# Linear attention's small products in the banks of scores and transposes, weights' splits in another order, head norms by logarithm and exponential

## The chip, the cores and the metric

One core of one Trainium2 chip. The metric is the device time of one execution in microseconds (us), the median of 3 runs; less is better.

## The reference, cut to what matters

Two transformer blocks in fp32 on 512 positions of width 1024. The first has forgetting attention and differential attention. The output of the latter is normed for each head, `y * rsqrt(mean(y*y) + eps) * gain`, and gated. The second block has block attention with relative positions (`moba_attention`) and gated linear attention side by side, then a cross attention to 256 memory rows and a 4096-wide MLP. The part that the change is about:

```python
def body(S, inp):                     # gated linear attention, one chunk
    qi, ki, vi, gi = inp
    b = jnp.cumsum(gi.astype(jnp.float32), axis=2)
    o_inter = jnp.einsum('bhcd,bhde->bhce', qf * jnp.exp(b), S)
    ...
    A = jnp.einsum('bhid,bhjd,bhijd->bhij', qf, kf, decay)
    o_intra = jnp.einsum('bhij,bhje->bhie', A, vf)
    ...
o_g = rms_norm_2(o_g, g_norm[l]).reshape(B, T, G_WIDTH) * jax.nn.silu(rg)
```

There are 4 heads with keys of 64 and values of 128.

## The kernel before

Five engines run their own instruction lists, written out by hand and tied by semaphores; `Plan` only counts groups and steps, so that each engine knows which value of a semaphore to wait for. There is no scheduler: an engine does its list in order, and whatever stands behind a waiting instruction waits too.

**Large products.** fp32 products are made of three float32r matmuls (`three`, lines 748 to 750): high by high, low by high, high by low. Weights come in halves of 512 KB through two raw buffers (`w_raw`, issued by SP's queue, line 561). ScalarE writes each half's high part (`split_hi`, line 1243), VectorE its low part (`split_lo`, by `lo_part`, line 1855) into four slots. A raw buffer is loaded again when VectorE has made the low part of the half before the last; a slot is free when the product that used it is done. `next_hi(name, n)` and `next_lo(name, n)` split the half four places behind half n of `name`. A product is either `t_product` (one half, one bank, 24 matmuls of 512 columns) or `m_quarters` (four halves, four banks, 24 matmuls for each quarter; `behind(q)` issues other work after quarter q). All of them write the four PSUM banks `lin` in turn: `claim(g)` makes TensorE wait until the group four before it has been read.

**Scores, transposes, head sums.** Four other banks, `sc` and `tr` with two each, hold attention scores and transposed probabilities; `sum_bank(h)` names them as four. They are used by the attentions, by the transposes of a norm's output and by the head sums (`head_sum`, line 797), and not by linear attention's products.

**Linear attention.** The four tiles of 128 positions are handled at once. `cross` (line 1085) computes the score blocks between different tiles, 6 for each head, in two groups for each head. Inside a tile a block is found on seven levels, `LEVELS = [64, 32, 16, 8, 4, 2, 1]`, and an eighth for the diagonal: at each level VectorE makes the distances to the middle of each block (`level_distance`, lines 2206 and 2207), ScalarE their exponential (`level_exp`, line 1607), VectorE the operands (`level_operands`, lines 2217 and 2218), TensorE 16 products of 128 by 128 with 64 rows (line 1105), and VectorE copies each head's entries under the level's mask into `g_a` (`level_scores`, line 2226). Ahead of all this stands the decay's logarithm: ScalarE takes an exponential on line 1326 and a logarithm on line 1327, and the first exponential after it on line 1611. Both `cross` and `levels` are groups of `lin`. Between levels stand large products, `rg` after each odd level and `ka2` after levels 2 and 4. The two `qa2` products stand ahead of `cross`. After the levels come `gla_pv` (line 1118, scores times values), and then `va2`, with two head sums behind each of its quarters 0 and 1.

**The order of splits around it.** VectorE makes the distances of levels 0 to 3 and the operands of levels 0 and 1 first, and then the four low parts due during `vg`. ScalarE has its high parts behind the exponentials, too, and the copies of `vg` to `g_v` behind the third one.

**Head norms.** For each of the two (in the first block for `y_1` of differential attention, in the second for linear attention) ScalarE squares the heads (line 1335), TensorE sums over partitions by a product with ones, ScalarE takes the square root (`head_roots`, line 1343), VectorE inverts it (line 1943) and multiplies (line 1944). There are two buffers for roots, so ScalarE's third and fourth root wait for the first two products of VectorE. In the second block ScalarE then waits for all four (`y_norm` 8), and only then come the splits and value tiles of `va2` (`v_heads`, lines 1353 and 1936), on both engines, ahead of the block attention's loop. In that loop each step has a score, an exponential, transposes of an earlier step, and a part of a large product as filling.

## Time and profile before

| | |
|---|---|
| Median of 3 runs | 1315.74 us (1313.95 to 1317.02) |
| The profiled execution's own time | 1315.0 us |
| Its span | 1313.2 us, mean granted clock 0.981 |
| TensorE busy (matmuls) | 1237.2 us, 94% |
| VectorE busy | 696.9 us, 53% |
| ScalarE busy | 549.6 us, 42% |
| Largest named wait of VectorE | 237.6 us before `w_lo`, for ScalarE's `w_hi` |

The profile names PE for TensorE's matmuls, PEld for its weight loads, DVE for VectorE, ACT for ScalarE, POOL for GpSimd. Times run from the span's start. An idle time is put down to the instruction that came last before it ended. Idle time on an engine that is not the bottleneck costs nothing.

### The profile page before, as it was taken

The numbers are of one execution on the slowest core, as the hardware profiler recorded it, in microseconds if no ns is written. First come the engines' busy times: TensorE is split into PE (matmuls) and PEld (weight loads), VectorE is DVE, ScalarE is ACT, GpSimd is POOL, SyncE is SP. The second block draws the span as 40 slices with busy tenths as digits, with TensorE's granted clock in tenths as the row PEclk, the third lists the DMA queues.
The fourth block names the chain that finished last, engine by engine and source line by source line (L and its number), as shares of the span: only waits on it lengthen the run. The fifth ranks groups of instructions, "written<-read, shape, count | busy, mean of one in ns | idle before, by whom it ended". The sixth has DMA issues, their size and how long they took to land.

```text
span 1313.2 us, 16539 instructions
## 1 busy us (share of the span) xinstructions
PE 1237.2 (94%) x6162; PEld 1026.9 (78%) x6162; DVE 696.9 (53%) x1047; ACT 549.6 (42%) x943; POOL 119.0 (9%) x193
## 2 busy tenths in 40 slices
PE   7999999999999989788888999999999999999996
PEld 5877887777888787666677789887798888888885
DVE  5556566865333557463657657444654343443433
ACT  5456685654332434422266545342343232231321
POOL 2023122200000010000014110010000000000000
PEclk9999999999999999899989999999999999999999
DMA  5312233113334342331023145510323332323321
GB/s 175 102 49 59 71 97 96 32 34 96 97 97 158 113 162 54 92 113 48 17 64 113 65 144 163 160 62 16 97 85 108 97 96 96 96 97 96 95 96 64
DMA packets 148227, 120.64 MB, mean 92 GB/s; under 512 B 4866, under 2 KB 123714, under 8 KB 148163
## 3 DMA queue, kind: packets, MB, share of 16 engines
q1 hardware_dynamic: 142672, 106.05, 27.1%
q10 hardware_dynamic: 5490, 13.73, 3.0%
q8 instruction: 41, 0.67, 0.2%
q14 instruction: 24, 0.19, 0.0%
HBM read 115.55 MB, written 4.22 MB: 91 GB/s over the span
## 4 chain that ended last, share of the span: by engine, by line
PE 80%; DVE 11%; ACT 4%; DMA 2%; issue 2%; POOL 0%; ACTq 0%; DVEq 0%; SPq 0%
PE lin L748 24%; PE lin L750 23%; PE lin L749 23%; DVE w_lo L1855 2%; PE tr L904 2%; DMA x_m<-in_x 1%; ACT w_hi L1243 1%; PE sc L914 1%; DVE g_z L1943 1%; DVE t_r L1943 1%; PE sc L916 1%; PE tr L897 1%; DMA w_raw<-in_w_in 1%; PE lin L940 1%; DVE neg_max L1880 1%
## 5 line engine op out<-in xcount | busy, mean ns | idle before, releaser
L1855 DVE TENSOR_TENSOR w_lo<-w_raw,w_hi 128x1024 fp32r<-128x1024 f32 x194 | 237.4, 1229 | 248.4 <-ACT w_hi L1243 237.6
L748 PE MATMUL lin<-h_hi,w_hi 128*128 128x512 f32 (+1 forms) x848 | 328.8, 388 | 23.5 <-DVE v_hl L1936 8.2
L750 PE MATMUL lin<-h_hi,w_lo 128*128 128x512 f32 (+1 forms) x848 | 320.4, 378 | 0.0
L749 PE MATMUL lin<-h_lo,w_hi 128*128 128x512 f32 (+1 forms) x848 | 320.4, 378 | 0.0
L1243 ACT ACTIVATE w_hi<-w_raw 128x1024 fp32r<-128x1024 f32 x194 | 203.8, 1054 | 244.3 <-PE lin L750 145.9
L748 PEld LDWEIGHTS lin<-h_hi,w_hi 128*128 128x128 f32 x848 | 162.4, 191 | 53.5 <-DVE v_hl L1936 8.4
L750 PEld LDWEIGHTS lin<-h_hi,w_lo 128*128 128x128 f32 x848 | 162.2, 191 | 29.6
L749 PEld LDWEIGHTS lin<-h_lo,w_hi 128*128 128x128 f32 x848 | 162.7, 192 | 25.5 <-issue 0.2
L748 PE MATMUL lin<-w_hi,u_hi 128*128 128x512 f32 x256 | 99.6, 389 | 0.0
L749 PE MATMUL lin<-w_lo,u_hi 128*128 128x512 f32 x256 | 99.6, 389 | 0.0
L750 PE MATMUL lin<-w_hi,u_lo 128*128 128x512 f32 x256 | 99.6, 389 | 0.0
L1880 DVE TENSOR_REDUCE neg_max<-sc 128x1 f32<-128x128 f32 (+3 forms) x112 | 52.3, 478 | 76.7 <-PE sc L916 57.0
L748 PE MATMUL lin<-w_hi,h_hi 128*128 128x512 f32 x192 | 77.8, 405 | 4.4 <-DVE h_lo L1855 4.2
L750 PE MATMUL lin<-w_hi,h_lo 128*128 128x512 f32 x192 | 75.7, 394 | 0.0
L749 PE MATMUL lin<-w_lo,h_hi 128*128 128x512 f32 x192 | 75.7, 394 | 0.0
L1285 ACT ACTIVATE p<-sc,neg_max 128x128 f32<-128x128 f32 (+1 forms) x80 | 42.2, 527 | 76.9 <-DVE neg_max L1880 75.1
L623 POOL TENSOR_SCALAR p<-p,rden 128x128 f32<-128x128 f32 (+1 forms) x80 | 53.8, 673 | 163.4 <-DVE rden L1884 115.2
L750 PEld LDWEIGHTS lin<-w_hi,u_lo 128*128 128x128 f32 x256 | 48.1, 188 | 10.0
L748 PEld LDWEIGHTS lin<-w_hi,u_hi 128*128 128x128 f32 x256 | 48.1, 188 | 9.9
L749 PEld LDWEIGHTS lin<-w_lo,u_hi 128*128 128x128 f32 x256 | 48.1, 188 | 9.9
L2449 DVE SCALAR_TENSOR_TENSOR u_f<-lin,relu 128x512 f32<-128x512 f32 x32 | 22.1, 691 | 61.3 <-ACT relu L1789 61.3
L617 POOL TENSOR_TENSOR rstd<-var,minus_half 128x1 f32<-128x1 f32 x22 | 13.0, 593 | 446.2 <-DVE var L1835 446.2
(300 smaller groups left out, 1943.8 us busy)
## 6 DMA issues: line engine op xcount, KB each, us to landing
w_raw<-in_w_in SPq DMA_DIRECT2D x74, 512.0 KB, 3.9
w_raw<-in_w_up SPq DMA_DIRECT2D x32, 512.0 KB, 4.0
w_raw<-in_w_down SPq DMA_DIRECT2D x32, 512.0 KB, 3.6
w_raw<-in_w_out SPq DMA_DIRECT2D x16, 512.0 KB, 3.6
w_raw<-in_w_xkv SPq DMA_DIRECT2D x16, 512.0 KB, 4.0
w_raw<-in_w_branch SPq DMA_DIRECT2D x8, 512.0 KB, 3.7
w_raw<-in_w_xq SPq DMA_DIRECT2D x8, 512.0 KB, 4.2
w_raw<-in_w_xo SPq DMA_DIRECT2D x8, 512.0 KB, 3.6
```

The lines of the kernel that those rows point to most:

```text
L623: pool.tensor_scalar(p, p, rden[:, s:s + 1], 1.0, ALU.mult, ALU.mult).then_inc(s_norm, 1)
L748: pe.matmul(o, lh, rh, start=start, stop=False)
L749: pe.matmul(o, lh, rl, start=False, stop=False)
L750: return pe.matmul(o, ll, rh, start=False, stop=stop)
L897: mm = pe.transpose(tr[:, r % 2, P * b:P * b + P], src[:, c:c + P], ident[:, :])
L904: mm = pe.transpose(tr[:, r % 2, P * j:P * j + P], src(j), ident[:, :])
L1243: act.activation(w_hi[u % SLOTS][:, :], w_raw[u % 2][:, :], ACT.Copy).then_inc(w_hi_s, 1)
L1285: act.activation(p, sc[:, s % 2, 0:n], ACT.Exp, bias=neg_max[:, s:s + 1], accum_out=denom[:, s:s + 1]).then_inc(s_exp, 1)
L1855: return dve.tensor_tensor(out, x, as_f32(hi), ALU.subtract)
L1880: dve.reduce_max(neg_max[:, s:s + 1], sc[:, s % 2, 0:n], AX, negate=True).then_inc(s_max, 1)
L1943: link(dve.reciprocal(root[:, h % 2, :], root[:, h % 2, :]))
L2449: dve.scalar_tensor_tensor(u, bank(g), 0.0, r, ALU.max, ALU.mult).then_inc(dve_evac, 1)
```

## The change

- `cross`, `levels` and `gla_pv` leave the groups of `lin`. They write `sum_bank(0)` to `sum_bank(3)`, and have semaphores of their own (`cross_done`, `cross_read`, `level_done`, `level_read`, `pv_done`, `pv_read`).
- TensorE's order: `cross` of two heads ahead of each `qa2` product, a large product behind each of levels 0 to 5 (`ka2`, `rg`, `ka2`, `rg`, `rg`, `rg`), level 6 ahead of `va2`, the diagonal level behind `va2`'s quarter 0, `gla_pv` behind quarter 1, all four head sums behind quarter 2.
- VectorE makes the low parts due during `vg` between the distances and operands; in the levels the masked copies come first, then the split and the rest of `ka2` or `qa2`, then operands and distances. ScalarE has two high parts ahead of the first exponentials.
- Head norms: `exp(-0.5 * ln(mean + eps))` on ScalarE, for four heads each function in turn, written over the squares. VectorE only multiplies. In the second block the square is read from PSUM, the gating with `g_gain` moves into steps 2 to 5 of the block attention's loop, and two of VectorE's norms stand behind its value tiles.

```diff
@@
     return fill, head


-KEYS_IN_LEVEL = {2: 0, 4: 1}
+BEHIND_LEVEL = [("ka2", 0), ("rg", 0), ("ka2", 1), ("rg", 1), ("rg", 2), ("rg", 3)]
 BY_TILES = [(0, 0), (0, 1), (1, 0), (1, 1), (0, 2), (0, 3), (1, 2), (1, 3)]

@@
-    p.group("cross", "A", 8)
-    for lev in range(len(LEVELS) + 1):
-p.group("levels", "D", 4)
-if lev % 2 == 1:
-    p.t_halves("rg", "A")
-elif lev in KEYS_IN_LEVEL:
-    p.t_halves("ka2", "AD")
-    p.group("gla_pv", "A", 4)
+    for name, _ in BEHIND_LEVEL:
+p.t_halves(name, "A" if name == "rg" else "AD")
     p.m_quarters("va2", "AD")
     p.attention("moba_pv", "AD", 32, 1, "moba")
@@
     def head_sum(h, squares, n):

         pe.wait_ge(sq_t, 4 * n + h + 1)
+        if n == 1:
+            pe.wait_ge(pv_read, h + 1)
         pe.matmul(sum_bank(h), ones[:, :], squares, start=True, stop=True).then_inc(sum_t, 1)

@@ TensorE @@
-    t_groups("qa2", 0, 2, hh, hl)
-    pe.wait_ge(gz_done, 1)
-    for h in range(4):
+    def cross_scores(h):
+
         rows = slice(HD * (h % 2), HD * (h % 2) + HD)
         kd, kx, qe = B["g_kd"][rows, h // 2, :], B["g_kx"][rows, h // 2], B["g_qe"][rows, h // 2, :]
...
-            g = G["cross"][2 * h + part]
-            claim(g)
-            for n, (key, i) in enumerate(pairs):
-                mm = pe.matmul(lin[:, g % 4, P * n:P * n + P], key, qe[:, P * i:P * i + P],
+            n = 2 * h + part
+            if n >= 4:
+                pe.wait_ge(cross_read, n - 3)
+            for c, (key, i) in enumerate(pairs):
+                mm = pe.matmul(sum_bank(n % 4)[:, P * c:P * c + P], key, qe[:, P * i:P * i + P],
                                start=True, stop=True)
-            mm.then_inc(lin_step, 1)
-    for lev in range(len(LEVELS) + 1):
+            mm.then_inc(cross_done, 1)
+    def level_products(lev):
+
+        if lev < len(LEVELS):
+            pe.wait_ge(gz_done, lev + 2)
...
+            heads = (2 * pair, 2 * pair + 1)
+            for h in heads:
+                if lev == 0:
+                    pe.wait_ge(cross_read, 5 + h)
                 else:
-                    keys_l.append(B["g_k"][rows, h // 2, :])
-                    queries_l.append(B["g_q"][rows, h // 2, :])
+                    pe.wait_ge(level_read, 4 * (lev - 1) + h + 1)
...
+                    mm = pe.matmul(sum_bank(h)[:, c], k[:, c], q[:, c], start=True, stop=True)
...
-                        mm.then_inc(lin_step, 1)
-        if lev % 2 == 1:
-            t_product("rg", lev // 2, 0, KT, hh, hl)
-        elif lev in KEYS_IN_LEVEL:
-            t_product("ka2", KEYS_IN_LEVEL[lev], 0, KT, hh, hl)
...
+                        mm.then_inc(level_done, 1)
+
+    def gla_values():
+        for h in range(4):
+            pe.wait_ge(cross_read, 8)
+            pe.wait_ge(level_read, 4 * len(LEVELS) + h + 1)
+            for j in range(NT):
+                mm = pe.matmul(sum_bank(h)[:, P * j:T], B["g_v"][:, j, P * h:P * h + P],
+                               B["g_a"][:, h, T * j:T * j + T - P * j], start=(j == 0), stop=(j == NT - 1))
+            mm.then_inc(pv_done, 1)
+
+    pe.wait_ge(gz_done, 1)
+    pe.wait_ge(sums_read, 4)
+    for pair in range(2):
+        for h in (2 * pair, 2 * pair + 1):
+            cross_scores(h)
+        t_groups("qa2", pair, pair + 1, hh, hl)
+    for lev, (name, n) in enumerate(BEHIND_LEVEL):
+        level_products(lev)
+        t_groups(name, n, n + 1, hh, hl)
+    level_products(len(LEVELS) - 1)
+
+    def rest_of_gla(q):
+        if q == 0:
+            level_products(len(LEVELS))
+        elif q == 1:
+            gla_values()
+        elif q == 2:
+            for h in range(4):
                 head_sum(h, B["g_d"][:, h // 2, h % 2, :], 1)

-    m_quarters("va2", 0, 0, hh, hl, behind=rest_of_norm)
+    m_quarters("va2", 0, 0, hh, hl, behind=rest_of_gla)

@@ ScalarE @@
         for h in range(4):
             act.wait_ge(sum_t, 4 * n + h + 1)
-            if h >= 2:
-                act.wait_ge(y_norm, 4 * n + h - 1)
-            act.activation(root[:, h % 2, :], sum_bank(h), ACT.Sqrt, scale=1.0 / P, bias=eps)\
-                .then_inc(sums_read, 1)
+            act.activation(root(h), sum_bank(h), ACT.Ln, scale=1.0 / P, bias=eps).then_inc(sums_read, 1)
+        for h in range(4):
+            act.wait_ge(sums_read, 4 * n + h + 1)
+            act.activation(root(h), root(h), ACT.Exp, scale=-0.5).then_inc(root_done, 1)
...
@@
         act.wait_ge(gd_done, n + 1)
         act.activation(B["g_d"][:, n], B["g_d"][:, n], ACT.Exp).then_inc(ge_done, 1)
     act.activation(g_tail[:, :, :], B["g_b"][:, :, P - 1:T:P], ACT.Exp).then_inc(ge_done, 1)
+    def cross_out(h):
+
+        n = 2 * h
+        act.wait_ge(cross_done, n + 1)
+        act.activation(B["g_a"][:, h, P:4 * P], sum_bank(n % 4)[:, 0:3 * P], ACT.Copy).then_inc(cross_read, 1)
+        act.wait_ge(cross_done, n + 2)
+        c = PT_STRIDE + 2 * P
+        act.activation(B["g_a"][:, h, c:c + 2 * P], sum_bank(n % 4 + 1)[:, 0:2 * P], ACT.Copy)
+        c = 2 * PT_STRIDE + 3 * P
+        act.activation(B["g_a"][:, h, c:c + P], sum_bank(n % 4 + 1)[:, 2 * P:3 * P], ACT.Copy)\
+            .then_inc(cross_read, 1)
+
+    for q in range(2):
+        next_hi("vg", q)
     for lev in range(2):
         level_exp(lev)
-    for q in range(3):
-        next_hi("vg", q)
+    next_hi("vg", 2)
     for t in range(NT):
         copy_lin(G["vg"][t], B["g_v"][:, t, :])
     next_hi("vg", 3)
     act.wait_ge(beta_out, 32)
-    for c in range(2):
-        queries_hi("qa2", c)
-        next_hi("qa2", c)
-    for lev in range(2, 4):
-        level_exp(lev)
     act.wait_ge(gla_const, 1)
-    for h in range(4):
-        g = G["cross"][2 * h]
-        step(g)
-        act.activation(B["g_a"][:, h, P:4 * P], lin[:, g % 4, 0:3 * P], ACT.Copy).then_inc(act_evac, 1)
-        step(g + 1)
-        c = PT_STRIDE + 2 * P
-        act.activation(B["g_a"][:, h, c:c + 2 * P], lin[:, (g + 1) % 4, 0:2 * P], ACT.Copy)
-        c = 2 * PT_STRIDE + 3 * P
-        act.activation(B["g_a"][:, h, c:c + P], lin[:, (g + 1) % 4, 2 * P:3 * P], ACT.Copy)\
-            .then_inc(act_evac, 1)
-    for lev in range(len(LEVELS) + 1):
+    for pair in range(2):
+        for h in (2 * pair, 2 * pair + 1):
+            cross_out(h)
+        level_exp(2 + pair)
+        queries_hi("qa2", pair)
+        next_hi("qa2", pair)
+    for lev, (name, n) in enumerate(BEHIND_LEVEL):
         if lev + 4 < len(LEVELS):
             level_exp(lev + 4)
-        if lev % 2 == 1:
-            copy_lin(G["rg"][lev // 2], B["y_0"][:, lev // 2, :])
-            next_hi("rg", lev // 2)
-        elif lev in KEYS_IN_LEVEL:
-            keys_hi("ka2", KEYS_IN_LEVEL[lev])
-            next_hi("ka2", KEYS_IN_LEVEL[lev])
+        if name == "rg":
+            copy_lin(G["rg"][n], B["y_0"][:, n, :])
+        else:
+            keys_hi(name, n)
+        next_hi(name, n)
         if lev == 1:
             bias_tiles_in()
     act.wait_ge(act_evac, AN[G["rg"][3]])
     act.activation(B["y_0"][:, :, :], B["y_0"][:, :, :], ACT.Silu).then_inc(rg_silu, 1)
+    for q in range(2):
+        next_hi("va2", q)
     for h in range(4):
-        copy_lin(G["gla_pv"][h], B["y_1"][:, h, :])
-    act.wait_ge(act_evac, AN[G["gla_pv"][3]])
-    head_squares(B["y_1"], lambda h: B["g_d"][:, h // 2, h % 2, :])
-    head_roots(1, B["g_z"][:, 0], eps_n[:, 1:2])
-    act.wait_ge(y_norm, 8)
-    v_heads("va2")
+        act.wait_ge(pv_done, h + 1)
+        act.activation(B["g_d"][:, h // 2, h % 2, :], sum_bank(h), ACT.Square).then_inc(sq_t, 1)
+        act.activation(B["y_1"][:, h, :], sum_bank(h), ACT.Copy).then_inc(pv_read, 1)
+    next_hi("va2", 2)
+    head_roots(1, lambda h: B["g_d"][:, h // 2, h % 2, :], eps_n[:, 1:2])
+    values_hi("va2")
+    next_hi("va2", 3)

     def moba_exps(m):
@@ VectorE @@
-    def head_norms(n, y, root):
-        for h in range(4):
-            dve.wait_ge(sums_read, 4 * n + h + 1)
-            link(dve.reciprocal(root[:, h % 2, :], root[:, h % 2, :]))
-            dve.tensor_tensor(y[:, h, :], y[:, h, :], root[:, h % 2, :], ALU.mult).then_inc(y_norm, 1)
+
+    def head_norms(n, y, root, heads=range(4)):
+        for h in heads:
+            dve.wait_ge(root_done, 4 * n + h + 1)
+            dve.tensor_tensor(y[:, h, :], y[:, h, :], root(h), ALU.mult).then_inc(y_norm, 1)

     def split_y(n, k):
@@
         s = LEVELS[lev]
         dve.wait_ge(ge_done, lev + 4)
         if lev >= 2:
-            step(G["levels"][4 * (lev - 2) + 3])
+            dve.wait_ge(level_done, 4 * (lev - 2) + 4)
         e_first, e_second = halves(B["g_d"][:, lev % 2], s)
         z_first, z_second = halves(B["g_z"][:, lev % 2], s)
         dve.tensor_tensor(z_first, e_first, halves(B["g_k"][:, :, :], s)[0], ALU.mult)
@@

     def level_scores(lev):
         for h in range(4):
-            g = G["levels"][4 * lev + h]
-            step(g)
+            dve.wait_ge(level_done, 4 * lev + h + 1)
             if lev > 0:
-                dve.wait_ge(dve_evac, DN[G["levels"][4 * (lev - 1) + h]])
+                dve.wait_ge(level_read, 4 * (lev - 1) + h + 1)
             dve.copy_predicated(diagonal(B["g_a"], h),
                                 B["g_mask"][:, lev:lev + 1, :].to_broadcast([P, NT, P]),
-                                bank(g).rearrange("p (t q) -> p t q", q=P)).then_inc(dve_evac, 1)
+                                sum_bank(h).rearrange("p (t q) -> p t q", q=P)).then_inc(level_read, 1)


     last = B["g_b"][:, :, P - 1:T:P].rearrange("p t (n o) -> p t n o", o=1)
@@
         dve.tensor_scalar(kx[:, 1, :], kx[:, 0, :], g_tail[:, dt, 2:3], None, ALU.mult)
         ins = dve.tensor_scalar(kx[:, 2, :], kd[:, P:2 * P], g_tail[:, dt, 2:3], None, ALU.mult)
     ins.then_inc(gz_done, 1)
+    next_lo("vg", 0)
     for lev in range(2):
         level_distance(lev)
+    next_lo("vg", 1)
     dve.wait_ge(gla_in, 48)
     for lev in range(2):
         level_operands(lev)
+    next_lo("vg", 2)
     for lev in range(2, 4):
         level_distance(lev)
-    for q in range(4):
-        next_lo("vg", q)
-    for c in range(2):
-        queries_lo("qa2", c)
-        next_lo("qa2", c)
+    next_lo("vg", 3)
+    queries_lo("qa2", 0)
+    next_lo("qa2", 0)
+
+    def behind(lev):
+
+        name, n = BEHIND_LEVEL[lev - 1] if lev > 0 else ("qa2", 1)
+        if name == "qa2":
+            queries_lo(name, n)
+        elif name == "ka2":
+            keys_lo(name, n)
+        next_lo(name, n)
+
     for lev in range(len(LEVELS)):
         level_scores(lev)
+        behind(lev)
         if lev + 2 < len(LEVELS):
             level_operands(lev + 2)
         if lev + 4 < len(LEVELS):
             level_distance(lev + 4)
-        if lev % 2 == 1:
-            next_lo("rg", lev // 2)
-        elif lev in KEYS_IN_LEVEL:
-            keys_lo("ka2", KEYS_IN_LEVEL[lev])
-            next_lo("ka2", KEYS_IN_LEVEL[lev])
     level_scores(len(LEVELS))
-    next_lo("rg", 3)
-    head_norms(1, B["y_1"], B["g_z"][:, 0])
-    dve.wait_ge(y_norm, 8)
+    for q in range(3):
+        next_lo("va2", q)
     dve.wait_ge(rg_silu, 1)
-    for h in range(4):
+    roots = lambda h: B["g_d"][:, h // 2, h % 2, :]
+    head_norms(1, B["y_1"], roots, range(2))
+    values_lo("va2")
+    head_norms(1, B["y_1"], roots, range(2, 4))
+    next_lo("va2", 3)
+
+    def gla_gate(h):
+        dve.wait_ge(y_norm, 5 + h)
         y = B["y_1"][:, h, :]
-        link(dve.scalar_tensor_tensor(y, y, g_gain[:, :], B["y_0"][:, h, :], ALU.mult, ALU.mult))
-    v_heads("va2")
+        dve.scalar_tensor_tensor(y, y, g_gain[:, :], B["y_0"][:, h, :], ALU.mult, ALU.mult)

     def moba_max(m):
         causal_max("moba")(m)
+        if 2 <= m < 6:
```

## Rows read from the trace of the kernel before

**Rows 1.** The page's first part: busy time, share of the span, instructions.
```profile
PE 1237.2 (94%) x6162; PEld 1026.9 (78%) x6162; DVE 696.9 (53%) x1047; ACT 549.6 (42%) x943; POOL 119.0 (9%) x193
```

**Rows 2.** TensorE's waits, 500 to 662 us: total, times, longest.
```profile
PE lin L748 <- DVE v_hl L1936: 8.2, 1, 8.2
PE lin L748 <- DVE g_a L2226: 6.0, 5, 1.8
PE lin L748 <- ACT g_v L1331: 4.6, 1, 4.6
PE lin L1105 <- DVE qk L1855: 3.6, 2, 1.8
```

**Rows 3.** Stretches: length, busy (instructions) by engine, granted clock, DMA, GB/s.
```profile
307.50:464.00 156.50, 153.17 (x682) 126.14 (x680) 67.76 (x82) 53.19 (x76) 2.21 (x4) 1.00 0.41 120
529.00:533.00 4.00, 4.00 (x12) 3.13 (x11) 1.61 (x2) 2.02 (x4) 0.00 (x0) 0.57 0.47 131
546.00:553.50 7.50, 7.27 (x55) 7.28 (x56) 1.26 (x2) 3.53 (x12) 0.00 (x0) 0.54 0.26 70
655.50:666.00 10.50, 5.68 (x16) 4.68 (x17) 5.44 (x9) 6.25 (x11) 0.37 (x1) 0.51 0.56 174
666.00:700.00 34.00, 33.98 (x193) 29.46 (x191) 19.84 (x49) 20.45 (x52) 10.47 (x15) 1.00 0.11 35
304.00:308.00 4.00, 3.79 (x10) 3.08 (x11) 1.23 (x1) 0.63 (x2) 0.00 (x0) 0.57 0.64 163
500.00:662.00 162.00, 134.76 (x747) 107.94 (x746) 93.56 (x116) 57.82 (x80) 6.60 (x12) 0.94 0.23 64
```

**Rows 4.** VectorE in order of time: start, length, instructions, idle before.
```profile
522.04 2.35 DVE L1855 TENSOR_TENSOR w_lo<-w_raw,w_hi 128x1024 fp32r<-128x1024 f32 x2
...
574.50 1.39 DVE L1855 TENSOR_TENSOR qk<-lin,qk 64x512 fp32r<-64x512 f32 x2 [2.71 <-ACT qk L1280]
...
577.17 2.59 DVE L2226 COPY_PREDICATED g_a<-g_mask,lin 128x512 f32<-128x512 int32 x4
579.64 0.69 DVE L2217 TENSOR_TENSOR g_z<-g_d,g_k 128x512 f32<-128x512 f32 x1
```

**Rows 5.** ScalarE in order of time, at the copies of `vg`.
```profile
527.07 1.06 ACT L1243 ACTIVATE w_hi<-w_raw 128x1024 fp32r<-128x1024 f32 x1 [6.86 <-DMA w_raw<-in_w_in]
528.03 2.04 ACT L1331 ACTIVATE g_v<-lin 128x512 f32<-128x512 f32 x4
```

**Rows 6.** TensorE in order of time: one level, `gla_pv`, two head sums.
```profile
563.90 2.12 PE L1105 MATMUL lin<-g_z 64*128 64x128 f32 x32
...
617.06 8.79 PE L1118 MATMUL lin<-g_a,g_v 128*128 128x512 f32 x32
...
631.15 1.88 PE L797 MATMUL sc<-g_d,ones 128*128 128x512 f32 x4
```

**Rows 7.** All engines in order of time around the second norm's end.
```profile
632.92 3.35 DVE L1943 RECIPROCAL g_z<-g_z 128x512 f32<-128x512 f32 x1 [12.87 <-ACT g_z L1343]
...
649.00 2.01 ACT L1243 ACTIVATE w_hi<-w_raw 128x1024 fp32r<-128x1024 f32 x2 [7.23 <-DVE y L1944]
...
657.35 1.06 ACT L1243 ACTIVATE w_hi<-w_raw 128x1024 fp32r<-128x1024 f32 x1 [6.33 <-DMA w_raw<-in_w_in]
...
659.58 2.47 DVE L1936 TENSOR_TENSOR v_hl<-lin,v_hl 128x512 fp32r<-128x512 f32 x4
...
660.32 0.80 PE L748 MATMUL lin<-h_hi,w_hi 128*128 128x512 f32 x1 [8.21 <-DVE v_hl L1936]
```

**Rows 8.** ScalarE and TensorE in order of time behind the first norm.
```profile
301.17 0.60 ACT L1522 ACTIVATE t_g<-lin 128x512 f32<-128x512 f32 x1
...
304.21 0.77 PE L748 MATMUL lin<-y_hi,w_hi 128*128 128x512 f32 x1 [2.25 <-DVE w_lo L1855]
```

**Rows 9.** ScalarE's table loads around the decay's logarithm.
```profile
500.31 1.28 ACT L1327 ACT_TABLE_LOAD   x1
...
504.21 1.28 ACT L1611 ACT_TABLE_LOAD   x1
```

More of the change, by code:

```diff
@@ L446, in two_blocks_kernel @@
         sums_read = sem("sums_read")
+        root_done = sem("root_done")
+        cross_done = sem("cross_done")
+        cross_read = sem("cross_read")
+        level_done = sem("level_done")
+        level_read = sem("level_read")
+        pv_done = sem("pv_done")
+        pv_read = sem("pv_read")
         y_hi_s = sem("y_hi_s")
@@ L715, in _ @@
                 keys_of("ka2", 2, c)
-            pool.wait_ge(lin_step, ST[G["gla_pv"][3]])
-            pool.wait_ge(y_norm, 8)
+            pool.wait_ge(pv_done, 4)
             empty_rows(2, range(4, 8))
@@ L1101, in _ @@
                     for t in range(NT):
                         c = slice(P * t, P * t + P)
-                        for n in range(2):
-                            g = G["levels"][4 * lev + 2 * pair + n]
-                            mm = pe.matmul(lin[:, g % 4, c], keys_l[n][:, c], queries_l[n][:, c], start=True, stop=True)
-                            if t == NT - 1:
-                                mm.then_inc(lin_step, 1)
-                if lev % 2 == 1:
-                    t_product("rg", lev // 2, 0, KT, hh, hl)
-                elif lev in KEYS_IN_LEVEL:
-                    t_product("ka2", KEYS_IN_LEVEL[lev], 0, KT, hh, hl)
@@ L1112, in _ @@
-            for h in range(4):
-                g = G["gla_pv"][h]
-                claim(g)
-                pe.wait_ge(act_evac, AN[G["cross"][2 * h + 1]])
-                pe.wait_ge(dve_evac, DN[G["levels"][4 * len(LEVELS) + h]])
-                for j in range(NT):
-                    mm = pe.matmul(lin[:, g % 4, P * j:T], B["g_v"][:, j, P * h:P * h + P],
-                                   B["g_a"][:, h, T * j:T * j + T - P * j], start=(j == 0), stop=(j == NT - 1))
-                mm.then_inc(lin_step, 1)
@@ L1122, in rest_of_norm @@
-            def rest_of_norm(q):
-                if q < 2:
-                    for h in (2 * q, 2 * q + 1):
+                        for h in heads:
+                            rows = slice(HD * (h % 2), HD * (h % 2) + HD)
+                            k, q = (B["g_z"][rows, lev % 2, pair, :],) * 2 if lev < len(LEVELS) else \
+                                (B["g_k"][rows, pair, :], B["g_q"][rows, pair, :])
+                            mm = pe.matmul(sum_bank(h)[:, c], k[:, c], q[:, c], start=True, stop=True)
+                            if t == NT - 1:
+                                mm.then_inc(level_done, 1)
```

40 lines of the change are left out of this document (18 added, 22 removed).

## The prediction

> **What bounds the kernel now.** I read the busy table first: TensorE has work in 94% of the span, VectorE in 53%, ScalarE in 42% [rows 1]. So TensorE's queue sets the end, and time can only come from stretches in which it stands still or runs at its lower clock. The busy share by stretches comes second. From 500 to 662 us, which is linear attention up to the first filling of the second block's attention, TensorE is busy for 134.76 of 162 us: it stands still for 27.2 us [rows 3]. The list of its waits in that stretch names the causes, the longest being 8.2 us for `v_hl`, 6.0 for `g_a`, 4.6 for `g_v` and 3.6 for `qk` [rows 2]. Third comes the granted clock [rows 3]: 1.00 through 156.5 us of dense work, but 0.57 in 529 to 533 (and once more for the 4 us after 597.5, a second such row), 0.54 in 546 to 553.5, and 0.51 in 655.5 to 666. Each of these follows waits. One more such place lies in the first block, at 304 to 308 us.
>
> **The reordered weights' splits.** The weight halves' low parts stand behind other work in VectorE's queue. Two of them start at 522.04 [rows 4], when the raw buffer they free is already wanted: the next DMA lands at about 527, ScalarE waits 6.86 us for it, and only behind that split does it empty the `vg` banks (528.03) [rows 5]. TensorE waits 4.6 us for one of those banks. The change puts the two splits ahead of the level distances and operands. Working forward from 514.7, where VectorE has finished the `g_kx` products: split to 515.9, its DMA (3.9 us, as from the end of the first of the two splits, 522.04 + 1.15, to 527.07 [rows 4, 5]) lands near 520, ScalarE's high part ends near 521 and the four `g_v` copies follow each product as it ends (the last at 523.9). The small products of heads 0 and 1 need none of those banks, so TensorE goes on at 523.9. The wait of 4.6 us goes.
>
> **Small products in their own banks.** Before, `cross` and `levels` share four banks with the large products, so a large product behind a level claims a bank whose small product VectorE has not read yet, and the small products claim one that still holds `qk`. That is the 6.0 and 3.6 us of waits [rows 2] and some shorter ones: 27.2 - 8.2 - 4.6 = 14.4 us in all. Afterwards level n + 1 waits only for the reads of level n, and a large product of 24 matmuls lies between: 24 x 156.5/682 = 5.5 us [rows 3]. One level is 32 short matmuls, 2.12 us [rows 6], so TensorE's period is 7.6 us. VectorE's work in the fullest period is four masked copies 2.59, two operands and two distances (four at 0.69, some 0.6 from start to start) 2.4, a weights' low part 1.15 (half of the pair's 2.35) and the keys' or queries' low part 1.39: 7.5 us [rows 4]. That is nearly the whole period, but the copies come first in it: they are read about 3 us before TensorE wants the bank. Operands are made two levels ahead, and from the third level on the period's work falls to 6.3 and less. I count this wait at nothing; with the cover gone (each of the first four levels 2 us late) it would cost 8 us. ScalarE's cross copies (six for two heads, none longer than the 0.6 us of a 512-column copy) lie under the 5.5 us of a `qa2` product.
>
> The two products of values and head sums only move. Four groups of `gla_pv` keep their 8.79 us, the head sums their 1.88 us for each two [rows 6]; the former now run between two quarters of `va2`. No matmul is added or taken away. SP's queue sees the same 512 KB loads in another order; the wait for POOL's memsets moves from the norm to `pv_done`, some 15 us before they are needed.
>
> **Norms by logarithm and exponential.** Before, VectorE inverts four roots, 3.35 us each; ScalarE stands behind `y_norm` until 649.00, so the last splits are late, the raw load for the next lands at 657, the `v_hl` parts follow it, and TensorE idles 8.2 us [rows 7]. When would TensorE come to that filling product without its stops? 660.3 - 27.2 of waits - 6.9 of clock (worked out below) = 626.2. One score (0.7), the last of `va2`'s quarters 0 to 3 (5.5) and four head sums (3.5) lie ahead of it, so quarter 2 ends at 616.5. ScalarE from there, by the rows' durations: high split to 617.8, table load 1.28 to 619.1, four logarithms at some 0.58 to 621.4, another load to 622.7, four exponentials to 624.7, then `v_hl` tile 0 to 625.3; VectorE's low part of it (0.68) ends at 626.0. TensorE wants that bank at 626.2, so the 8.2 us fall to nothing, with 0.2 us to spare. But VectorE then has three more low parts, two norms and a split (1.9 + 1.2 + 1.2 us) ahead of the first row maximum, which ends at 630.6; with the exponential behind it the third score waits until 631.2, where TensorE is ready at 629.6. That is a new wait of 1.6 us. The four gating products (3.0 us) moved into the attention's steps 2 to 5 are covered: VectorE is busy 19.84 of the 34 us after 666 [rows 3].
>
> In the first block the same edit acts alone. VectorE's inversions end so late that the first sigmoid starts at 301.17, a weights' split follows it, and TensorE idles 2.25 us up to 304.21 and then runs at 0.57 [rows 3, 8]. ScalarE has four logarithms and four exponentials for four roots and one table load more (2.0 + 1.28 us), VectorE loses 13.4 us of inversions. From the sums' end at 279.6 (load, four logarithms, load, four exponentials, load and the long activation 1.9 us, four gatings, splits, load) my schedule has the sigmoid near 293.5: 7 us earlier, so the wait goes.
>
> **A rule on tables.** The rows show an exponential, a load of 1.28 us, a logarithm, and then a load of 1.28 us before the next exponential (L1611) [rows 9]: the two functions do not share a table as this program is built. I count two loads per norm from that row. The Trainium skill ("ScalarE: Activation LUTs", Table sets: the hidden batching unit) says that one set holds both, so that a logarithm followed by an exponential takes one load. By that rule each norm would be 1.28 us shorter; the trace disagrees.
>
> **The sum**, against the profiled execution's 1315.0 us (span 1313.2, 1.8 around it; the median shown is 1315.74, 0.7 more):
> - waits removed in 500 to 662: 27.2 us;
> - clock there: (4 + 4) x 0.43 + 7.5 x 0.46 = 6.9 us, and 5.68 us of work at 0.51 = 2.8 us;
> - first block: 2.25 + 4 x 0.43 = 4.0 us;
> - new wait at the third score 1.6 us, with a low clock behind it, since lows have followed waits of 2 us (304 us): 1.7 us.
> 27.2 + 6.9 + 2.8 + 4.0 - 3.3 = 37.6 us. So 1315.0 - 37.6 = 1277.4, and by the median 1278. After this stretch TensorE has no wait in 666 to 700 (33.98 of 34 busy), so what it gains is kept to the end.
>
> Ends of what no row shows: if all lows and the new wait vanish, 37.6 + 3.3 = 41 us, and the refills after each wait, which busy time hides, may give 2 us more: 1272. If half the clock's 9.7 us stays as lows elsewhere (5 us) and the new wait is 4 us, 1285. This is the likeliest case's own range.
>
> **Rivals.**
> - *The tail stays late.* Values' low parts stand behind a chain of two loads, eight activations and two norms, with 0.2 us to spare in my schedule. Against it: no inversion is left, and the raw loads no longer hang on it. If each link costs 0.3 us more, the bank comes 3 to 4 us late, and a low clock of 10 us (5 us lost, like the one after 655.5) follows: 8 us back, 1286.
> - *VectorE becomes the bound in the levels.* 7.5 of 7.6 us speaks for it, the order in the period against it. Six late levels at 2 us plus lows of 4: 16 us back, 1294.
> - *Shared tables.* If an exponential directly behind logarithms needs no load of its own, the tail is 1.28 us shorter, the third score's wait falls to 0.3 us and its low goes: 3 us better, 1275. Against it: the load at L1611, which stood behind a logarithm [rows 9]. This is what the rule of the Trainium skill named above would make of it.
> - *The clock takes it back.* TensorE's rests in 500 to 662 go; if the chip answers unbroken work there by the low level, then work of some 124 us between 502 and 626 runs at 0.5. From 76 us of low clock (38 lost) on, the kernel is slower; all of it costs 62 us: 1340. Against it: 156.5 us at 1.00 without a rest before that [rows 3]. For it: only that short 64-row matmuls at 546 ran at 0.54, which the waits before them explain.
> - *It does not do what it says:* the waits' banks turn out to be others, since only the last releaser is named; gain 10 us or less: 1306.
>
> **Chances.** Forecast 0.62, late tail 0.15, levels bound 0.09, shared tables 0.05, clock 0.04, no effect 0.05. The range for 8 in 10 holds the first two and shared tables: 1271 to 1292. Measurement tells 0.2% (2.6 us) from no change. Slower holds the clock case, 0.04; within 0.2% 0.02 of the no-effect case; faster the rest, 0.94.
>
> **What would show it.** Right: `claim`'s waits for `g_a`, `g_v` and `v_hl` absent from TensorE's list; clock 1.00 from 515 to 622; the first filling product near 622 on the new time axis (626 less the first block's 4); table loads twice at each norm; a wait of 1 to 2 us at a score with ScalarE's `p` named. Wrong: waits of levels for `g_a`, a `v_hl` wait above 3 us, DMA named before ScalarE's splits, or lows without waits ahead of them. The forecast falls if the stretch keeps more than 10 us of standing still.

## The result

The changed kernel takes 1276.39 us (median of 4 runs, 1273.11 to 1278.07) against 1316.38 us before (4 runs, 1313.95 to 1317.14): a ratio of 0.9696, 95% interval 0.9672 to 0.9720. That is 40.0 us or 3.0% less; 1278.0 us was predicted. The profiled execution took 1278.07 us, its span is 1276.3 us at a mean granted clock of 0.989, against 1315.0, 1313.2 and 0.981.

### The profile page after: what moved, and what is told of

Same layout as the page of the kernel before. It is cut to its first block, busy times and chain, and to the rows that moved or that the text cites. A ratio compares the mean times of both kernels' runs of the same rounds, so it can differ in the third digit from the quotient of the medians.

```text
span 1276.3 us, 16512 instructions
## 1 busy us (share of the span) xinstructions
PE 1226.8 (96%) x6162; PEld 1018.2 (80%) x6162; DVE 669.9 (52%) x1039; ACT 554.9 (43%) x952; POOL 119.0 (9%) x193
## 4 chain that ended last, share of the span: by engine, by line
PE 87%; DVE 6%; ACT 3%; DMA 2%; issue 1%; POOL 0%; ACTq 0%; DVEq 0%; SPq 0%
PE lin L748 26%; PE lin L750 25%; PE lin L749 25%; PE tr L906 2%; DVE w_lo L1877 2%; DMA x_m<-in_x 1%; PE sc L916 1%; PE sc L918 1%; PE tr L899 1%; ACT w_hi L1257 1%; PE lin L942 1%; DVE neg_max L1902 1%; DMA w_raw<-in_w_xkv 1%; PE lin L941 1%; DVE h_lo L1872 1%
```

## The profile after

The page's first part: TensorE has the same 6162 instructions, 96% instead of 94% busy; VectorE has 27.0 us less, mostly inversions, and ScalarE 5.3 us more [rows 1].

```profile
PE 1226.8 (96%) x6162; PEld 1018.2 (80%) x6162; DVE 669.9 (52%) x1039; ACT 554.9 (43%) x952; POOL 119.0 (9%) x193
```

TensorE's waits from 490 to 640 us, the same work as in [rows 2] (engine, line, what it waited for: total, times, longest). Of the `g_a`, `g_v` and `qk` waits nothing is left, and of 8.2 us for `v_hl` 0.4:

```profile
PE sc L916 <- ACT p L1299: 1.3, 1, 1.3
PE lin L748 <- DVE v_hl L1962: 0.4, 1, 0.4
```

Stretches that answer to [rows 3] (columns as there): the dense one of the first block, with no low clock behind the first norm any more; linear attention, 1.68 us without work where there were 27.24; its core at clock 1.00; and the low clock before the dense stretch that follows.

```profile
303.50:460.00 156.50, 153.50 (x683) 126.41 (x682) 66.47 (x80) 51.48 (x74) 2.20 (x4) 1.00 0.39 116
500.00:626.50 126.50, 124.82 (x742) 99.71 (x742) 77.79 (x111) 57.08 (x83) 6.61 (x12) 1.00 0.29 84
515.00:622.00 107.00, 106.63 (x661) 84.91 (x660) 59.17 (x82) 47.85 (x71) 4.53 (x8) 1.00 0.30 89
668.00:675.20 7.20, 5.04 (x19) 4.78 (x20) 5.98 (x13) 4.46 (x13) 3.54 (x2) 0.53 0.60 225
```

ScalarE in order of time, at the copies of `vg` (was [rows 5]): the raw weights now land 0.28 us after ScalarE is free, not 6.86, and the copies follow the products one by one.

```profile
515.74 1.06 ACT L1257 ACTIVATE w_hi<-w_raw 128x1024 fp32r<-128x1024 f32 x1 [0.28 <-DMA w_raw<-in_w_in]
516.70 0.58 ACT L1345 ACTIVATE g_v<-lin 128x512 f32<-128x512 f32 x1
...
520.21 0.60 ACT L1345 ACTIVATE g_v<-lin 128x512 f32<-128x512 f32 x1 [0.76 <-PE lin L750]
```

VectorE in the period of level 0, from one level's copies to the next (was [rows 4]): 7.84 us from start to start; no row between them, nor the last, has an idle time. That is more than the 7.5 us forecast, and more than TensorE's own 7.65 us (536.53 to 544.18), so VectorE falls behind by 0.2 us in this period and by 0.1 in the next (its copies start at 553.28, TensorE's level at 551.83). The copies end at 540.3, 3.9 us before TensorE's next level starts at 544.18, and that covers it.

```profile
537.72 1.37 DVE L2249 COPY_PREDICATED g_a<-g_mask,sc 128x512 f32<-128x512 int32 x2 [5.42 <-PE sc L1108]
538.98 1.34 DVE L2249 COPY_PREDICATED g_a<-g_mask,tr 128x512 f32<-128x512 int32 x2
540.35 1.39 DVE L1878 SCALAR_TENSOR_TENSOR qk<-lin,qk 64x512 fp32r<-64x512 f32 x2
...
545.56 1.38 DVE L2249 COPY_PREDICATED g_a<-g_mask,sc 128x512 f32<-128x512 int32 x2
```
```profile
544.18 0.97 PEld L1108 LDWEIGHTS sc<-g_z 64*128 64x128 f32 x16 [0.35 <-issue]
```

The second norm's end (was [rows 7]), ScalarE: two table loads, as predicted, on the way to the values' copies, then 2.68 us of waiting for the first row maximum.

```profile
613.08 1.28 ACT L1355 ACT_TABLE_LOAD   x1
614.38 1.27 ACT L1355 ACTIVATE g_d<-sc,eps_n 128x512 f32<-128x512 f32 x2
615.53 1.27 ACT L1355 ACTIVATE g_d<-tr,eps_n 128x512 f32<-128x512 f32 x2
616.82 1.28 ACT L1358 ACT_TABLE_LOAD   x1
618.11 2.20 ACT L1358 ACTIVATE g_d<-g_d 128x512 f32<-128x512 f32 x4
620.21 2.04 ACT L1365 ACTIVATE v_hl<-lin 128x512 fp32r<-128x512 f32 x4
622.12 1.07 ACT L1257 ACTIVATE w_hi<-w_raw 128x1024 fp32r<-128x1024 f32 x1
625.87 0.37 ACT L1299 ACTIVATE p<-sc,neg_max 128x128 f32<-128x128 f32 x1 [2.68 <-DVE neg_max L1902]
```

TensorE's weight loads at the two places where it still waits: the first filling product at 621.57, which before came at 660.32 (38.75 us later), and the third score.

```profile
621.57 0.19 PEld L748 LDWEIGHTS lin<-h_hi,w_hi 128*128 128x128 f32 x1 [0.52 <-DVE v_hl L1962]
626.38 0.19 PEld L916 LDWEIGHTS sc<-qk 128*128 128x128 f32 x1 [1.73 <-ACT p L1299]
```

## The experiments

Each was timed five times (e5 and e6 six times), on three chips; e1, e3, e4 and e6 share one, e2, e5, e7 and e8 another, the four others the third, each with its runs of the kernel before. "Clock loss" is the mean over a kernel's runs of span x (1 - granted clock), and "rest" is the mean of span x clock: what the span would be at full clock. A low clock during a wait costs nothing but is counted as a loss, and the rest is short by as much; 2.6 to 3.7 us of it lie behind TensorE's last work in every profile. Where it matters elsewhere it is said. The difference of one of e1 to e3 and e7 to e9 from the changed kernel, taken by their ratios, has a 95% interval of about 3 to 3.5 us to each side.

| kernel | median us | ratio to before (95%) | clock loss | rest |
|---|---|---|---|---|
| before (chip of e1, e3, e4, e6) | 1319.43 | 1 | 30.6 | 1287.0 |
| before (chip of e2, e5, e7, e8) | 1317.75 | 1 | 28.6 | 1287.7 |
| before (chip of the others) | 1319.10 | 1 | 29.7 | 1287.2 |
| changed, first measurement | 1276.39 | 0.9696 (.9672-.9720) | 12.1 | 1262.1 |
| changed, again | 1278.36 | 0.9694 (.9677-.9711) | 15.1 | 1262.0 |
| e1 first norm old | 1280.44 | 0.9713 (.9697-.9729) | 15.1 | 1264.6 |
| e2 splits old | 1281.25 | 0.9721 (.9701-.9740) | 14.3 | 1265.5 |
| e3 second norm old | 1287.29 | 0.9751 (.9737-.9766) | 17.2 | 1267.9 |
| e4 banks alone | 1296.43 | 0.9818 (.9804-.9832) | 22.0 | 1272.0 |
| e5 splits alone | 1310.54 | 0.9935 (.9912-.9958) | 25.1 | 1283.0 |
| e6 norms alone | 1307.04 | 0.9904 (.9884-.9923) | 22.0 | 1282.7 |
| e7 copies last | 1277.32 | 0.9689 (.9670-.9709) | 11.5 | 1263.8 |
| e8 maxima first | 1272.93 | 0.9657 (.9637-.9676) | 10.7 | 1261.0 |
| e8 again | 1274.45 | 0.9670 (.9650-.9691) | 12.7 | 1260.1 |
| e9 tables in turn | 1282.68 | 0.9735 (.9715-.9756) | 14.4 | 1267.3 |
| e10 banks old | 1298.22 | 0.9837 (.9811-.9864) | 18.1 | 1276.9 |

### One part undone

**e1, the first norm as before.**
```
-            head_roots(0, lambda h: B["t_sq"][:, h, :], ...)      # Ln, Exp
+            head_roots_old(0, lambda h: B["t_sq"][:, h % 2, :], ...)  # Sqrt; VectorE inverts
```


> The changed kernel with its first head norm as before: square root on ScalarE into two buffers in turn, reciprocal and product on VectorE; the second norm as changed. By step (d) the wait of 2.25 us before the products of the branch's first half comes back, with 1.7 us of low clock behind it: 4.0 us over the changed kernel (1280.4). Rival, the clock's part was counted twice, since the clock falls somewhere near this place anyway: 2.3 us over.


Measured 1280.44 us, its ratio 0.0019 (2.5 us) above the changed kernel's; the interval of the difference, about 3 us to each side, doesn't tell 4.0 from 2.3. The trace does for the wait: 2.24 us for `w_lo` are back at 305.29, with a low clock right behind.

```profile
305.29 0.66 PE L748 MATMUL lin<-y_hi,w_hi 128*128 128x512 f32 x1 [2.24 <-DVE w_lo L1884]
```
The rest rises by 2.6 us, which is about the wait; how much the clock adds stays unclear, since this run had no lows near 460 and 490, which the changed one has.

**e2, the splits as before.**
```
-            next_lo("vg", 0) ... distances ... next_lo("vg", 1) ... operands ... 2 ... 3
+            distances, operands, distances; for q in range(4): next_lo("vg", q)
             # ScalarE: all of next_hi("vg", 0..2) behind the two exponentials again
```


> The changed kernel with the splits of vg's four quarters back in the old order (ScalarE's three first splits behind the two first level exponentials, VectorE's four behind all distances and operands). If step (a) is a step of its own, the wait for the second quarter's rounded part comes back: 4.6 us of waiting on TensorE near 490, and up to 1.7 us of low clock behind it, so 4.6 to 6.3 us over the changed kernel (1281 to 1283). Rival, the splits only looked late because the level operands were urgent and in their own banks nothing wants them early: within 1 us of the changed kernel.


1281.25 us, by the ratios 3.4 us over the changed kernel, about 3.4 to each side: the timing alone tells neither the 4.6 to 6.3 expected nor the rival's 1 us from it. The trace does: the wait is back, but shorter than expected. `g_v` is as late as before, 34.43 us after the small product with `rp_table` in e2, 34.44 before, but TensorE waits 2.24 us for it and not 5.04: with banks of their own, the cross products of two heads run ahead of that wait and fill 2.8 us of it. TensorE's weight loads before, then in e2:

```profile
494.22 0.09 PEld L1070 LDWEIGHTS lin<-one_hot,rp_table 32*8 32x8 f32 x2 [0.76 <-issue]
...
528.66 0.19 PEld L748 LDWEIGHTS lin<-h_hi,w_hi 128*128 128x128 f32 x1 [5.04 <-ACT g_v L1331]
```
```profile
490.71 0.09 PEld L1072 LDWEIGHTS lin<-one_hot,rp_table 32*8 32x8 f32 x2 [0.76 <-issue]
...
520.48 0.29 PEld L1087 LDWEIGHTS sc<-g_qe,g_kd 64*128 64x128 f32 x2 [0.35 <-issue]
...
525.14 0.19 PEld L748 LDWEIGHTS lin<-h_hi,w_hi 128*128 128x128 f32 x1 [2.24 <-ACT g_v L1345]
```

**e3, the second norm as before** (four roots' buffers are kept).
```
-            head_norms(1, ...)   # y * root
+            head_norms_old(1, ...)   # reciprocal(root), y * root, four times
```


> The changed kernel with its second head norm by square root and reciprocal, on four buffers; first norm, banks and order as changed. ScalarE is ready earlier by one table load (1.28 us) and four exponentials (2.2 us), VectorE has 4 x 3.35 us of reciprocals more: the split of the values comes 2 to 3 us later than now (a wait of 2.6 instead of 0.4 us before the product that follows), and the row maximum at 625.6 comes near 635, so that the third score waits about 11 us in place of 1.7. With the clock behind that wait 9 to 14 us over the changed kernel (1285 to 1290). Rival, TensorE has filling products enough to go on with and only the first wait shows: 2 to 4 us over.


1287.29 us, 7.5 us over the changed kernel by the ratios (4.6 to 10.5), a little under the 9 to 14 expected, over the rival's 2 to 4 for the first wait alone. The row maximum comes at 634.81 as forecast. The third score's wait is 6.95 us, not 11: I had left out that TensorE gets there 4.0 us later, at 628.7 instead of 624.65: by 2.3 us of the longer first wait and by the low clock that stands behind it from 624 to 628 us, which costs 1.7. VectorE, then TensorE's weight loads in e3:

```profile
629.68 3.35 DVE L1980 RECIPROCAL g_d<-g_d 128x512 f32<-128x512 f32 x1
...
634.81 0.62 DVE L1909 TENSOR_REDUCE neg_max<-sc 128x1 f32<-128x128 f32 x2
```
```profile
624.04 0.19 PEld L748 LDWEIGHTS lin<-h_hi,w_hi 128*128 128x128 f32 x1 [2.84 <-DVE v_hl L1969]
635.64 0.28 PEld L916 LDWEIGHTS sc<-qk 128*128 128x128 f32 x1 [6.95 <-ACT p L1299]
```

### One part alone, and two without the third

**e4, the banks alone**: the changed kernel with the edits of e1, e2 and e3 together.


> The changed kernel with splits and both norms as before: what is left is the small products in banks of their own and the order of products and gates that goes with it. If the parts add up, it lies above the changed kernel by the sum of the three undone parts (about 4.0 + 5.5 + 11 = 20.5 us, 1297) and 19.6 us below the kernel before (14.4 us of waits and 5.2 us of clock). Rival, the waits hang together, so that one part's gain shows only with the others: no more than 12 us below the kernel before (1304 or more).

**e5, the splits alone**: the kernel before with the splits' order of the change (e2's edit, reversed).


> The kernel before with the splits' order alone changed, small products and norms as they were. By step (a) alone: 4.6 us of waiting and 1.7 us of low clock go, 1310 to 1312 against 1316.4. Rival, the operands of the levels come later by two splits of VectorE (2.35 us) and the level products that share the filling banks wait for them: no more than 2.5 us are left of the gain (1314 or more).

**e6, the norms alone**, in the kernel before:
```
-                    act.activation(root[:, h % 2, :], sum_bank(h), ACT.Sqrt, ...)
+                    act.activation(root(h), sum_bank(h), ACT.Ln, ...)   # then Exp, scale -0.5
+            for q in range(2): next_hi("va2", q)     # next_lo on VectorE, ahead of the norm
```


> The kernel before with both head norms by logarithm and exponential, and two splits of va2 moved ahead of the second one; banks and splits of vg as before, gates still ahead of the values. Step (d) gives 4.0 us. In the second norm the values would be ready near 647 where TensorE wants them at 652, so the whole wait of 8.2 us goes, with 2.8 us of clock: 15 us below the kernel before (1301.4), 14 to 17.5. Rival, the filling banks shared with the small products hold it back, and half of the 8.2 us comes up elsewhere: 8 to 10 us below.

**e10, splits and norms, the banks as before**: e5 and e6 together.


> The kernel before with the splits reordered and both norms by logarithm and exponential, but the small products still in the filling banks: the changed kernel without its first part, opposite to the kernel with the banks alone. By the rows of the two runs with one part each, waits of 5.2 (splits) and 8.4 us (norms) go and add up, so that TensorE's own time (span less what the low clock costs) falls by 13.6 us; 14 to 14.5 us of waits for g_a, qk and g_z stay between 535 and 610. In time about 1299 to 1302, some 22 us over the changed kernel. Rival, the norms' path gets late when the splits come early, or the other way round: more than 1304.

Against the kernel before on the same chip, by ratio: e4 24 us (22 to 26), e5 8.6 us (5.5 to 11.6), e6 12.7 us (10 to 15), e10 21.5 us (18 to 25). Each part pays by itself, so the rivals of e4 and e5, by which the waits hang together, fall. e4 gives more than the 19.6 us expected: its rest falls by 15.0 us where 14.4 of waits were forecast, its clock loss by 8.6 where 5.2 were. e6 gives less than its 14 to 17.5 and more than its rival's 8 to 10, and the interval reaches only the former; its trace has waits of 1.53 us for `v_hl` and 0.53 at the third score where none was expected. e10 came out at 1298.22 us, just under the 1299 to 1302 expected, but its rest falls by 10.3 us and not by 13.6. Some 2.3 us of what is lacking are the share of the old `v_hl` wait that the rest leaves out, since that wait lay in a low clock. The parts seem to overlap: alone they make 45 us, together 40, and the banks are worth 24.0 us alone but 18.9 by the ratios between e10 and the changed kernel. Each of these differences of 5 us has an interval of 4.5 to 5 us to each side, so timing hardly shows them. What shows an overlap is the trace of e2: 2.8 us of cover for `g_v`. More than that is not shown.

The traces show the expected waits. In e10 they are for the banks alone, 13.9 us (14.4 in the prediction; two of 1.1 and 0.8 are left out below), beside 1.4 for `v_hl`; the list of TensorE's waits there, 500 to 662 us:

```profile
PE lin L749 <- DVE g_a L2228: 5.9, 5, 1.8
PE lin L1106 <- DVE qk L1858: 3.6, 2, 1.8
PE lin L1106 <- DVE g_a L2228: 2.5, 2, 2.2
PE lin L749 <- DVE v_hl L1939: 1.4, 1, 1.4
...
```

and in e4 they are for the other two parts alone:

```profile
PE sc L916 <- ACT p L1299: 6.5, 1, 6.5
PE lin L748 <- DVE v_hl L1968: 2.7, 1, 2.7
PE lin L748 <- ACT g_v L1345: 1.8, 1, 1.8
```

### The order in a level, and the tail

**e7, copies last.**
```
             for lev in range(len(LEVELS)):
-                level_scores(lev)
                 behind(lev)
                 ... operands, distances ...
+                level_scores(lev)
```


> The changed kernel with VectorE's masked copies of a level behind the operands, distances and split of that period instead of ahead of them. The prediction put the smallness of the waits in the levels down to the copies coming first, since VectorE is busy 7.5 of 7.6 us in the periods of levels 0 to 2. If that is what saves them, copies come some 4.9 us later in each of these periods, the banks are free about 2 us after TensorE wants them, and the operands of the level after the next come 2.6 us earlier, which nothing needs: 3 to 6 us over the changed kernel, and waits for a copy near 537, 545, 553. Rival, the banks have a whole period of slack (the next level's products want them 7.65 us later) and the order doesn't matter: within 0.5 us.


1277.32 us, ratio 0.9689 against 0.9696 and 0.9694: no loss that timing can tell. VectorE's copies of level 0 end at 543.0, 9.1 us after that level's first weight load (533.88) instead of 3.8, and TensorE is back at 541.91. Yet it waits only 0.73 us where 0.35 is usual, and 0.22 us more before the second pair of heads. The banks are claimed pair by pair: the first pair's copies end at 541.8, the second pair's at 543.0, each just as TensorE comes to it.

```profile
540.42 1.37 DVE L2249 COPY_PREDICATED g_a<-g_mask,sc 128x512 f32<-128x512 int32 x2
541.68 1.34 DVE L2249 COPY_PREDICATED g_a<-g_mask,tr 128x512 f32<-128x512 int32 x2
```
```profile
541.91 1.00 PEld L1108 LDWEIGHTS sc<-g_z 64*128 64x128 f32 x16 [0.73 <-issue]
543.13 1.00 PEld L1108 LDWEIGHTS tr<-g_z 64*128 64x128 f32 x16 [0.22 <-DVE g_a L2249]
```
The periods of the first levels are 8.03, 8.01 and 7.71 us instead of 7.65: 0.8 us in all. So the theory's 3 to 6 us are refuted: it had set the last copy against the first claim. The rival's time comes out, but not its reason: with the copies last nothing is left of the period of slack.

**e8, maxima first.**
```
             values_lo("va2")
-            head_norms(1, B["y_1"], roots, range(2, 4))
-            next_lo("va2", 3)
             def moba_max(m):
                 causal_max("moba")(m)
+                if m == 1: head_norms(1, B["y_1"], roots, range(2, 4))
+                if m == 2: next_lo("va2", 3)
```


> The changed kernel with VectorE's last two norm products moved behind the second row maximum of the attention that follows, and the split of va2's last quarter behind the third. The third score of that attention waits 1.7 us for ScalarE's p, which waited 2.68 us for the row maximum behind these three (2.5 us of VectorE). The theory: that wait goes and nothing new comes, 1.5 to 2.0 us below the changed kernel (1274.6), the fastest version. Rival, the last quarter's split is then late for its product or the maxima of the following rows queue behind what was moved, and nothing is gained: within 0.5 us.

> The changed kernel once more, unaltered, so that the next three have it on the same chip. Its ratio to the kernel before is expected where it was, 0.967 to 0.972; 1276 to 1279 us.

> The kernel with VectorE's first row maxima ahead of the last norms again, now beside the changed kernel on the same chip. Its trace had the wait at the third score gone and nothing in its place. Theory: 1.7 us of waiting and, in most runs, one stretch of low clock less (1.7 us): 1.7 to 3.5 us below the changed kernel. Rival: the 5 us by which the two medians differed relative to the kernel before are the chip's or the clock's spread, and side by side they are within 1 us.


The first measurement of e8 lies 4.9 us below the changed kernel by the ratios, more than the 1.5 to 2.0 expected, but the two were timed on different chips. The changed kernel again came where it was expected. Side by side: 1274.45 (1272.88 to 1277.61) against 1278.36 us (1277.67 to 1281.43). The difference of the means is 4.2 us, 95% interval 1.7 to 6.7, a ratio of 0.9967. So the rival's 1 us falls, and the 1.7 to 3.5 us expected lie inside the interval. The wait at the third score is gone; the rest falls by 1.9 us (1.7 expected), the clock loss by 2.3 (1.7). It is the fastest of the versions. In the trace of the second measurement the maxima stand ahead of the norms, and 0.7 us of small waits for `pt_lo` have come in place of the one at the third score (0.2 us in the first):

```profile
618.23 2.48 DVE L1962 TENSOR_TENSOR v_hl<-lin,v_hl 128x512 fp32r<-128x512 f32 x4 [0.68 <-ACT v_hl L1365]
620.63 0.28 DVE L1902 TENSOR_REDUCE neg_max<-sc 128x1 f32<-128x128 f32 x1
621.16 0.42 DVE L1902 TENSOR_REDUCE neg_max<-sc 128x1 f32<-128x256 f32 x1 [0.25 <-PE sc L918]
621.50 1.29 DVE L1968 TENSOR_TENSOR y<-y,g_d 128x512 f32<-128x512 f32 x2
```
```profile
PE tr L906 <- DVE pt_lo L1911: 0.7, 2, 0.6
PE lin L748 <- DVE v_hl L1962: 0.4, 1, 0.4
```

**e9, tables in turn.**
```
-                for h in range(4): ... Ln;   for h in range(4): ... Exp
+                for h in range(4): ... Ln, Exp        # second norm only
```


> The changed kernel with the second norm's logarithm and exponential taken head by head, so that the function changes eight times in place of two: six more table loads of 1.28 us, 7.7 us, on ScalarE's path to the values' parts. If each change costs its load and that path is what TensorE waits for, the wait for v_hl grows from 0.5 to about 8.2 us, the one at the third score stays near 1.7, and with the low clock behind so long a wait (2.8 us as before the change) the kernel comes 8 to 12 us over the changed one. Rival, one table holds both functions and the two loads seen have another cause (the Square or the Copy ahead of them): no load more, within 0.5 us.


1282.68 us, 5.4 us over the changed kernel by the ratios (1.9 to 8.9), between the theory's 8 to 12 and the rival's nothing, which falls. The mechanism is the theory's: every change of function is a load of 1.28 us, eight of them, and the way from the first load to the values' copy grows from 7.13 to 15.66 us.

```profile
612.94 1.28 ACT L1359 ACT_TABLE_LOAD   x1
614.23 0.63 ACT L1359 ACTIVATE g_d<-g_d 128x512 f32<-128x512 f32 x1
614.88 1.28 ACT L1356 ACT_TABLE_LOAD   x1
...
624.06 0.69 ACT L1356 ACTIVATE g_d<-tr,eps_n 128x512 f32<-128x512 f32 x1
```
What I had wrong is where TensorE stands: 6.70 us before the first scores, only 2.10 before the filling product. The head sums lie in the scores' banks, and the first score starts right after the last logarithm has read them (624.06 + 0.69 us).

```profile
624.92 0.29 PEld L916 LDWEIGHTS sc<-qk 128*128 128x128 f32 x1 [6.70 <-issue]
...
627.95 0.29 PEld L748 LDWEIGHTS lin<-h_hi,w_hi 128*128 128x128 f32 x1 [2.10 <-DVE v_hl L1963]
```
While it stood there, the maxima caught up, so the third score doesn't wait. In all it waits 6.6 us more than in the changed kernel, and somewhat under half of the 10 us of low clock there (622 to 632) lies in the waits, where it costs nothing.

## Why the prediction was right

**What bounds it.** TensorE's queue. Standing still fell from 27.24 us [rows 3] to 1.68 us, and 2.25 us went in the first block [rows 8]: 27.8 us by the rows. The prediction's terms without the clock are 27.2 + 2.25 - 1.6 = 27.9 us. Over the whole span TensorE's time without work fell from 76.0 (1313.2 - 1237.2) to 49.5 us, by 26.5: 1.3 us of small gaps came elsewhere, 0.8 of them between 12 and 300 us.

**The clock.** TensorE's busy time fell from 1237.2 to 1226.8 us, by 10.4. With the 26.5 us above that makes the 36.9 us by which the spans differ. The low clock accounts for all of the 10.4: read in steps of 1 us, with the granted clock at 0.50 inside each low stretch, it costs TensorE's work 19.4 us before and 9.0 after, and in both profiles 1217.8 us of work at full clock remain (1215.7 to 1218.7 in all others). (Taking the losses of the whole spans, 25.0 and 14.0 us, would also count lows in which TensorE stands still.) The prediction has 6.9 + 2.8 + 1.7 - 1.7 = 9.7 us. That its whole sum, 37.6, comes within 0.7 us is partly luck, since its parts do not match one by one. The lows that it names are gone, 11.0 us. The kernel before had five more, of 3.4 us each, at 222, 464, 495, 710 and 894, which it leaves out; the one at 222 is missing after the change (1.5 us), though nothing there was changed, and the second profile of the changed kernel has 6.8 us of low clock at that place. Against this, the lows behind 662 us cost 2.2 us more than before: 6.8 and 3.4 us of low clock at 668 and 716, where the kernel before had only the 3.4 at 710. The low that the prediction put behind the new wait was not there. One of 6.8 us came at 668, 42 us later, around a stand of 2.76 us before a transpose that every profile of these kernels has:

```profile
670.13 0.29 PEld L906 LDWEIGHTS tr<-ident,p 128*128 128x128 f32 x2 [2.76 <-issue]
```
All five profiles with a wait of 1.73 us (1.71 in e2) at the third score show 6.8 us of low clock there, both of e8, without it, 3.4. That doesn't prove that the wait is the cause, but e8's gain fits.

**The splits.** The wait of 4.6 us went. The copies of `g_v` ended at 520.8, 0.9 us later than forecast (523.9 less the first block's 4.0). But the wait's worth is 4.6 only in the kernel before; beside the banks it is 2.2 on the weight loads (e2), since the prediction's own remark that the cross products need none of those banks already covers the rest.

**The banks.** 14.4 us of waits were forecast and 13.9 stand in e10. No level waits for VectorE, as said, though its work in the fullest period was sized too small: 7.84 us, not 7.5, and so longer than TensorE's 7.65. The reason given, that the copies come first, is worth 0.8 us and not the 8 us of the "cover gone" case (e7), since the banks are wanted pair by pair and even the last place in the period is just in time.

**The norms.** The first filling product was forecast near 622 and started at 621.57 after 0.4 us of waiting (forecast 0). The wait at the third score was 1.73 us on the weight loads and 1.3 on the matmuls (forecast 1.6), and its place, 626.4, is 0.8 us before 631.2 - 4.0. In the first block the first sigmoid ran at 294.01 (forecast 293.5).

**The tables.** Two loads per norm, as the row of before had it [rows 9]. The Trainium skill's rule ("ScalarE: Activation LUTs", Table sets: the hidden batching unit) that logarithm and exponential share a set doesn't hold in these programs; e9 has eight loads of 1.28 us for eight changes. Why the two functions are loaded apart here, no run shows.

**The rivals.** No wait for `g_a` at a level and no low clock in the 107 us from 515 on: VectorE as the bound, the clock and "doesn't do what it says" are all refuted. The late tail is there in kind, with 0.4 us of its 3 to 4.

## What to carry to other kernels

When a list of waits names several buffers, work out each wait's end with the others gone: the work that one edit lets run ahead covers part of another's wait (2.8 of 5.0 us in e2), and gains of parts need not add. In an engine's queue the short operation that a busy engine's next bank hangs on, here a row maximum of 0.28 us, belongs ahead of anything that nobody awaits; that was 4 us (1.7 to 6.7) for two moved lines. And weigh the granted clock as a cost of its own behind each wait, but don't count a low clock twice while the engine stands.

## What the runs showed of the hardware

The places of the low clock vary from run to run of one program: the changed kernel had 6.8 us at 221, 3.4 at 436 and 3.4 at 463 in its second profile, where the first had only 3.4 at 460. Both have a low at 490 to 494. That makes the clock loss of equal programs vary by 3 us (12.1 and 15.1 us), while the rest differs by 0.1 us (1262.1 and 1262.0). For e8, measured twice, the loss differs by 2.0 us and the rest by 0.9, and the kernel before has 2.0 and 0.7 over the three chips; so for effects of 2 us the rest is the better measure, as long as no wait lies in a low clock. A table load took 1.28 us every time, also right behind the activation that used the other table.
